# Later places in TensorE's queue for two modulation products, an earlier one for the gate-column product, in a one-core mLSTM and pooling layer

## The reference

```python
def _adaln(cvec, w, b):
    m = jax.nn.silu(cvec) @ w + b
    return jnp.split(m, 3, axis=-1)          # shift, scale, gate

def _hybrid_layer(x, xc, mod_x, mod_c, norm_w, in_w, ...):
    shift, scale, gate = [m[:, None, :] for m in mod_x]
    shift_c, scale_c, gate_c = mod_c
    parts_x = _split_proj((_rmsnorm(x, norm_w) * (1 + scale) + shift) @ in_w)
    parts_c = _split_proj((_rmsnorm(xc, norm_w) * (1 + scale_c) + shift_c) @ in_w)
    ...                                       # mLSTM in both directions, pooling mixer
    x = x + gate * _merge(parts_x, y_m, y_p, out_w)
    return x, xc
```

## Time and profile before

| | us |
|---|---|
| median of three runs | 2402.42 |
| the profiled execution's own time | 2401.29 |
| its span, first to last instruction | 2399.5 |
| PE busy | 2274.2 (95%) |
| DVE busy | 1494.0 (62%) |
| ACT busy | 972.8 (41%) |
| POOL busy | 610.1 (25%) |
| mean granted TensorE clock | 0.98 of full speed |

### The profile page before, as it was taken

The page is one execution under the profiler, slowest core; times in us unless marked ns, Lnnn a source line. Parts: engine busy times, 40 slices in busy tenths (PEclk is TensorE's granted clock), DMA queues, the critical chain, the costliest instruction groups (busy, mean ns, idle before and its releaser), DMA issues. The chain is left out here.

```text
span 2399.5 us, 35270 instructions
## 1 busy us (share of the span) xinstructions
PE 2274.2 (95%) x12251; PEld 1934.1 (81%) x12251; DVE 1494.0 (62%) x2660; ACT 972.8 (41%) x1982; POOL 610.1 (25%) x545
## 2 busy tenths in 40 slices
PE   7799999989999989999999999999999699999998
PEld 5588888767887878888888888888887488888878
DVE  5545567875766646575767566767675355646564
ACT  6323355542332323434444344444443535252532
POOL 0223344533445421121122112321220212020210
PEclk9899999999999999999999999999999799999999
DMA  9466698876788666666776877666665665757562
GB/s 273 143 154 176 180 250 242 255 218 136 192 201 249 163 223 224 222 221 215 233 250 201 274 262 250 224 221 200 227 211 188 206 192 158 234 171 226 187 207 100
DMA packets 399266, 501.66 MB, mean 209 GB/s; under 512 B 25800, under 2 KB 283380, under 8 KB 393588
## 3 DMA queue, kind: packets, MB, share of 16 engines
q1 hardware_dynamic: 334836, 377.76, 48.0%
q10 hardware_dynamic: 55136, 83.90, 14.0%
q0 software_dynamic: 9120, 37.75, 6.0%
HBM read 352.82 MB, written 163.27 MB: 215 GB/s over the span
## 5 line engine op out<-in xcount | busy, mean ns | idle before, releaser
L1867 PE MATMUL bank<-xlate,wh 128*128 128x512 f32 x2048 | 670.4, 401 | 10.1 <-DVE v_t L2001 6.3
L1867 PEld LDWEIGHTS bank<-xlate,wh 128*128 128x128 f32 x2048 | 373.1, 189 | 79.4 <-DVE v_t L2001 6.7
L1867 PE MATMUL bank<-xlate,wl 128*128 128x512 f32 x1024 | 409.6, 400 | 0.0
L1016 PE MATMUL bank<-xlate,wh 128*128 128x512 f32 x1024 | 330.4, 396 | 5.8 <-DVE wl L1288 4.9
L1016 PE MATMUL bank<-xtop,wh 128*128 128x512 f32 x768 | 250.6, 403 | 9.9 <-DVE wl L1288 9.9
L1016 PEld LDWEIGHTS bank<-xlate,wh 128*128 128x128 f32 x1024 | 191.1, 189 | 48.1 <-ACT wh L1068 4.7
L1867 PEld LDWEIGHTS bank<-xlate,wl 128*128 128x128 f32 x1024 | 193.4, 189 | 34.1
L1016 PE MATMUL bank<-xlate,wl 128*128 128x512 f32 x512 | 201.4, 393 | 0.0
L1016 PEld LDWEIGHTS bank<-xtop,wh 128*128 128x128 f32 x768 | 144.2, 192 | 41.8 <-ACT wh L1068 10.8
L2024 DVE SCALAR_TENSOR_TENSOR state<-state,cols,bank 128x516 f32<-128x516 f32 x128 | 95.7, 748 | 112.0 <-PE bank L1828 111.9
L1016 PE MATMUL bank<-xtop,wl 128*128 128x512 f32 x384 | 152.7, 398 | 0.0
(11 more groups left out here) (321 smaller groups left out, 5351.4 us busy)
## 6 DMA issues: line engine op xcount, KB each, us to landing
v_t<-vk_d SPq DMA_DIRECT2D x144, 384.0 KB, 3.8
qk_d<-os SPq DMA_DIRECT2D x32, 1024.0 KB, 5.7
q_t<-qk_d SPq DMA_DIRECT2D x128, 256.0 KB, 4.1
wraw<-wpair_d ACTq DMA_DIRECT2D x31, 1024.0 KB, 6.6
rawb<-in_in_w_dram ACTq DMA_DIRECT2D x64, 256.0 KB, 5.4
vk_d<-os SPq DMA_DIRECT2D x16, 1024.0 KB, 4.6
wpair_d<-in_in_w_dram POOLq DMA_DIRECT2D x64, 256.0 KB, 6.1
k_t<-qk_d SPq DMA_DIRECT2D x64, 256.0 KB, 5.0
```

Source lines behind the costliest of these rows:

```text
L1016: mm = pe.matmul(dst[:, :], a[:, kd, :], x_block(part, XB[name])[:, kd], start=(kd == 0 and n == 0), stop=(kd == KH - 1 and n == 2))
L1867: mm = pe.matmul(bank[m % 2][:, :], a[:, u % 2, k, :], xlate[part][:, BLOCK_OF[k // KH, tq], k % KH], start=(k == 0 and n == 0), stop=(k = ...
```

## The change

Two edits. In stage 1, modulations 4 and 5 and the turn of row 4 no longer stand on PE between the token transposes s = 1 and s = 2 of kd = 0; they follow s = 3, ahead of modulations 6 and 7, and ACT's copies of rows 4 and 5 move behind its work for s = 3 in the same way. In stage 2, the product with ones moves from position MG + 14 to MG + 12 on PE, and what DVE does with it from MG + 15 to MG + 13. Nothing is added or removed.

```diff
@@ PE, stage 1
                         turn_x(4 * kd + s, range(QT1 * (s // 2), QT1 * (s // 2) + QT1), kd + KH * (s % 2))
 
-                        if kd == 0 and s == 1:
-                            modulation(4)
-                            modulation(5)
-                            turn_row(4)
                         if 1 <= kd < KH - 1:
...
                     if kd == 0:
-                        for i in (6, 7):
+                        for i in range(4, 8):
                             modulation(i)
-                            turn_row(i - 1)
+                            if i > 4:
+                                turn_row(i - 1)
                     if kd + 1 < KH:
                         turn_row(4 * (kd + 1) + 3)
@@ ACT, stage 1
-                            if kd == 0 and s == 1:
-                                copy_row(4)
-                                copy_row(5)
...
                     if kd == 0:
-                        for i in (6, 7):
+                        for i in range(4, 8):
                             copy_row(i)
@@ stage 2, the bound on positions, PE, and DVE
-            assert MG + 17 < AT[NU - 1, "M6"]
+            assert MG + 16 < AT[NU - 1, "M6"]
...
-                    if p == MG + 14:
+                    if p == MG + 12:
...
-                    if p == MG + 15:
+                    if p == MG + 13:
                         dve.wait_ge(mg_done, 1)
```

## The result

The changed kernel took 2416.54 us, the kernel before 2402.86 (medians of six executions each; one of the changed kernel's six was disturbed, at 9078.24, and is in no ratio: the other five go from 2412.39 to 2419.11): a ratio of 1.0051, 95% interval 1.0038 to 1.0065. Three of the six of the kernel before are those behind its 2402.42. The forecast was 2409.2, at most 2412.5. So the sign was right and the size too small. The profiled execution of the changed kernel took 2414.57, its span 2412.8, which is 13.3 us more than the span of the kernel before (2399.5).

The account below looks back on a forecast made before the run. PE, busy 95% of the span, was taken to bound the kernel. The stage 1 edit's +3.7 us and the stage 2 edit's +3.1 make +6.8, added to the earlier kernel's median for 2409.2 us; range 2404.0 to 2412.5.

Parts of the forecast that it names:

- Stage 1 ends as late as the row turns: Stage 1: a later last row turn for kd = 1, then at 36.47 us, is not caught up before stage 2.
- Rival 4: Stage 1: the transposes were the limit, so their earlier start reaches the end; sum -4.9 us, 2397.5 us; chance 0.05.
- A = +3.7: Stage 1 edit: the last row turn for kd = 1 comes at 40.2 us instead of 36.5, +3.7 us.
- The Trainium skill's rule on the transposes: Stage 1: transposes don't count as busy for the clock, so it rises near 36.3 us, not 34.1; edit's cost +4.8 us.
- rival 3: Stage 1: the load of weight piece 8 lands late; sum +11.3 us, 2413.7 us; chance 0.08.
- rival 2: Stage 1: the clock comes back at once, so that edit costs +1.1 us; sum +4.2, 2406.6 us; chance 0.08.
- rival 1: Stage 2: sums end sooner, the product with ones fits PE's hole, -1.8 us; sum +1.9, 2404.3 us; chance 0.13.
- B, the waiting: +2.1: Stage 2 edit: PE waits for the eighth sum until 782.8 us instead of for `wl` until 780.71, +2.1 us.
- B, the clock: +1.0: Stage 2 edit: half clock of 4.1 to 6.0 us behind the longer hole loses 2.0 to 3.0 us, 1.0 more than before.
- The sum: Whole kernel: +3.7 us from the stage 1 edit and +3.1 from the stage 2 edit make +6.8 us.
- The base: Whole kernel: the median of three executions of the kernel before, to which the +6.8 us was added for 2409.2 us.
- My own sign of failure: Stage 2: the distance from its start near 80 us to 770 us changing by over 1 us would mean the forecast is wrong.

Follow-up runs that it names:

- e3: The kernel before, unchanged, run again as a control; 2405.38 us, ratio 0.9999.
- e4: The kernel before with the product with ones one position earlier (MG + 13), not two, stage 1 unchanged; 2405.8 us, ratio 1.0009 to the kernel before.
- e8: The kernel before with unused filler matmuls in PE's holes in stage 1 and ahead of product 211; 2405.52 us, ratio 1.0002 to the kernel before.
- e9: The kernel before with the sums of `mga` on every second position and the product with ones behind them at MG + 19; 2401.72 us, ratio 0.9983.
- e10: The kernel before with the sums of `mga` spaced out and filler matmuls in stage 1's holes; 2404.34 us, ratio 0.9996 to the kernel before.
- e5: The changed kernel again, unedited, twelve executions beside 34 of the kernel before; 2414.82 us, ratio 1.0033 to the kernel before.
- e1: The changed kernel with only the stage 1 edit, the product with ones at its old place; 2408.6 us, ratio 1.0018 to the kernel before.
- e7: The changed kernel with twenty unused matmuls ahead of the product with ones' wait for the sums; 2411.11 us, ratio 1.0016 to the kernel before.
- e11: The changed kernel with seven of the eight sums, so the product with ones waits only for the seventh; 2410.91 us, ratio 1.0020 to the kernel before.
- e2: The kernel before with only the stage 2 edit, the product with ones moved to MG + 12; 2411.11 us, ratio 1.0020 to the kernel before.
- e6: The changed kernel with unused filler matmuls in PE's holes in stage 1; 2416.04 us, ratio 1.0036 to the kernel before.
- e12: The kernel before with half the stage 1 edit: modulation 5 and row 4's turn behind s = 3, modulation 4 left in place; 2406.84 us, ratio 1.0006.

## Why the forecast came out too small

- **Stage 1 ends as late as the row turns** (right). (b) is 43.69 before and 43.69 after, and PE's only waits from 32 to 62 us in the changed kernel are the 0.6 us of the earlier trace rows. It holds for later row turns; when they are earlier than in the first profile of before, weight loads take a part back (e3, e4, e8, e9, e10). Rival 4, that the transposes were the limit, falls by that.
- **A = +3.7** (nearly right in size, in part by luck). The last row turn stood at 39.46, not 40.2. The transposes started at 28.81, not 28.1, since the inputs were 0.7 us later (DVE's scaling there starts at 26.0, before at 25.34; the first transposes, ahead of the edit, were 0.6 us later too), and the clock rose at 32.3, 3.5 us after PE resumed, not 6.0. In e5 it took about 5.9: two modulations at full speed take 3.66, these took 5.66, so 4.0 us of them were at half, up to 34.6. Over the five profiles with edit A and stage 1 unfilled (changed, e1, e5, e7, e11) the mean of (a) is 16.6, over the five with the old order (before, e2, e3, e4, e9) 13.1: +3.6. Forecast were 17.7 and 13.98: the 6.0 us of half clock made both about 1 us too long, and that cancels in the difference. The first pair alone would say +2.4, because the profile of before had one of its longer half clocks. What counts for the end is the start of stage 2: (a) and (b) together are 60.3 in the mean of the same five with edit A and 57.0 in that of the five without, **+3.3**; the 0.3 us between come from e3, e4 and e9, with their waits for weights.
- **The Trainium skill's rule on the transposes** ("TensorE: Matmul & The Clock Gate", PE-mode transpose) would by the 6.0 us of the earlier trace rows put the rise 6.0 us behind the last transpose (28.81 + 1.97 = 30.8). The row shows it at 32.3, 1.5 us behind the last transpose and 3.5 behind the first. That is no support for the rule, but with a recovery that itself goes from 3.5 to 5.9 us in one kernel it isn't a refutation; no experiment here separated the two.
- **Piece 8 of the weights late** (rival 3, false). No wait for `aw` stands in the changed kernel between 32 and 62 us.
- **The clock no obstacle in stage 1** (rival 2, false): 6.7 us at 0.50, of which PE was busy for 3.5. Its own end at full clock, 37.6, adds up to 37.5 by the terms it names; e6 took 9.0 us from these transposes to the last row turn, which from 28.1 makes 37.1.
- **The ones in the hole** (rival 1, false as the kernel stands, and true of its place once the eighth sum is left out): e11's -1.5 for its -1.8. That the last sum is long because it runs beside POOL's work is right (see the last section).
- **B, the waiting: +2.1** (right). 4.71 for 2.57, and 4.7 in all four profiles that have edit B, eight sums and no fill ahead of the ones.
- **B, the clock: +1.0 (wrong in size, the step that failed in the prediction's own sum).** I let the half clock behind the longer hole last 4.1 to 6.0 us, the times found at other holes. It lasted 6.3 in the first profile and 8.0 in e2 and e5: 3.1 to 4.0 us lost against 1.6 before. The product with ones takes 3.57 of it, twice 1.84, since it now is the first thing behind the hole. The mean of (d) over changed, e2, e5 and e6 is 18.5, against the 14.26 of above: **B = +4.3**, not +3.1. Less the 2.1 of waiting that is 2.1 us for the clock where the sum had 1.0, and e7, which fills the hole, gives 2.2 of them back.
- **The sum.** 3.28 + 4.25 = +7.5 us, a ratio of 1.0031, inside e5's interval. The mechanism was right, the sum 0.7 us short: B had 1.1 too little, A 0.4 too much.
- **The base** (a term of the forecast that was low by the later sessions). I added to 2402.42, the median of three executions. The level is 2405.6, so the base was 3.2 us low by it, which is more of the miss of 7.3 us than the sum's 0.7. 2405.6 + 7.5 = 2413.1 would have been the forecast; the changed kernel has 2414.8 in e5 and 2416.5 in the first comparison. But beside the first comparison's own 2402.86 the base was only 0.4 low: whether its few executions lay low by chance, or that session was faster, no run shows.
- **My own sign of failure**, the distance from the start of stage 2 to 770 us, came: (c) grew by 4.8. It was a bad sign, because it takes an unchanged kernel to hold still; before and e3, the same kernel, differ by 1.6, and before and e12 by 4.3. Theory 2, a carry-over, isn't borne out by the means (696.8 and 697.8), but 1 us of it could hide in this scatter.
- **What stays open.** Of the first comparison's 12.3 us (1.0051), 7.5 are shown in place. Of the other 4.8, 2.1 are that the six executions of the kernel before had a mean of 2403.5, below the level; the rest is the scatter of few executions, or a cost that I can't place. The two intervals, 1.0038 to 1.0065 and 1.0021 to 1.0045, overlap a little; e5's, 5 to 11 us, holds the 7.5, the first one's, 9 to 16 us, doesn't.

## What to carry to other kernels

Ahead of a position that an engine is to reach earlier, look at what stands before the awaited instruction on the producer: moving the consumer ahead of one product put it in front of the producer's last 2.3 us sum, and spacing the producer's sums out won about what moving the consumer lost. Needed work that fills a wait costs nothing that could be measured, even at half clock (e12). A gain ahead of a point where loads can set the pace is to be followed to the next stage, and not only to the step that was sped up (e8, e10). And before adding a forecast of 0.3% to a base, take the base from many executions, and its parts from more than one profile.

## What the runs showed of the hardware

- The time at half clock behind the same hole is not fixed: 3.5 and 5.9 us in stage 1 and 6.3 and 8.0 behind the ones, in two profiles of one kernel whose waits agree to 0.02 us. Over the 35 executions of the kernel before beside e1 to e4, time and mean granted clock (0.975 to 0.983) correlate at -0.80, in the two later sessions at -0.71 and -0.55; half of PE's busy time in all half-clock stretches is 27.3 us in the first profile of before and 34.1 in that of the changed kernel. The Trainium skill, "TensorE: Matmul & The Clock Gate", What's actually happening, says that the number of matmuls at half clock varies from run to run of one kernel (6, 11 or 14 at its start). These rows agree, for holes within a kernel.
- Behind the same wait the clock does not always fall: ahead of product 211 PE waits 2.5 to 2.6 us in before, e1, e3, e4 and e12; in four of them 3.4 us at half clock begin between 0.1 us before it resumes and 1.4 us after, in e1 none do.
- In e7 the clock fell at 790.3 for 3.3 us though PE was busy for 7.57 of the 7.70 us before; the 16 matmuls of two columns lay just ahead. So a fall to half clock doesn't always mark a hole in PE's work.
- DVE's sum of 128x1024 elements took 1.28, 2.30 or 3.83 us in the same kernel. The long ones came in the same order in the kernels that have all eight sums in the old positions (3.85, then 2.30 before; 3.83, then 2.28 in the changed kernel), so the forecast of the wait, which rests on them, held. In e9, with the sums spaced, the third, fifth, seventh and eighth were the long ones (2.33, 3.81, 2.32, 2.32).
- What makes them long is POOL, by these traces. Each of these eight long sums (two in before, two in the changed kernel, four in e9) runs beside one or two `TENSOR_TENSOR` of POOL, the first of which started before it or at most 0.2 us behind it, and ends 1.1 us behind the end of that work. A sum that meets none takes 1.28, and so does one where POOL's starts over 1 us behind it (779.82 in the changed kernel). Beside the sum of before that starts at 774.96 and ends at 778.81 POOL has these:

```profile
775.15 1.31 POOL L902 TENSOR_TENSOR ssum<-ssum,rawb 128x512 f32<-128x512 f32 x1
776.41 1.30 POOL L906 TENSOR_TENSOR ssum<-rawb 128x512 f32<-128x512 f32 x1
```

They keep their 1.3 us, and DVE is done 1.10 us behind 777.71; in the same way the last sum is done 1.09 us behind POOL's end at 781.74. So 1.0 of the 2.3 us of the sum that edit B waits for is waiting for POOL, as the prediction's rival 1 supposed. But its way out, a start of DVE ahead of POOL's, is not borne out by this row: DVE's start is recorded 0.19 us ahead of POOL's, and it waited all the same.
